# Stick-breaking attention: scores copied out of their bank by ScalarE, suffix sums added by VectorE, no second score matmul

## What is computed

```python
z = jnp.einsum('bqhd,bshd->bhqs', qb, k_b).astype(f32) * scale
strict = (key_pos[None, :] < t[:, None])[None, None]
log_1mb = jnp.where(strict, jax.nn.log_sigmoid(-z), 0.0)
after = lax.cumsum(log_1mb, axis=3, reverse=True) - log_1mb
att = jnp.where(strict, jnp.exp(jax.nn.log_sigmoid(z) + after), 0.0)
ob = jnp.einsum('bhqs,bshd->bqhd', att.astype(v_b.dtype), v_b)
```

## Time and profile before

| | us |
|---|---|
| median of 3 runs | 1699.08 |
| lowest, highest | 1697.08, 1699.22 |
| the profiled execution | 1696.48 |
| its span, first to last instruction | 1694.7 |
| TensorE busy | 1578.8 (93%) |
| VectorE busy | 840.5 (50%) |
| ScalarE busy | 624.2 (37%) |

### The profile page before, as it was taken

One profiled execution on the slowest core, in us unless ns is written; L12 is line 12 of the kernel. 1 busy time (PEld: TensorE's weight loads), 2 busy tenths in 40 slices (PEclk: granted clock), 3 DMA queues, 4 the chain that ended last, 5 costly groups with the idle time before them and its releaser, 6 DMA issues.

```text
span 1694.7 us, 22877 instructions
## 1 busy us (share of the span) xinstructions
PE 1578.8 (93%) x9177; PEld 1226.9 (72%) x9177; DVE 840.5 (50%) x1545; ACT 624.2 (37%) x1109; POOL 592.1 (35%) x452
## 2 busy tenths in 40 slices
PE   5899999999899988899899999998899899999997
PEld 4688766777788666677677776666677877877776
DVE  3779366333426356633518995455474533222224
ACT  4232365453322245443234324554353322221222
POOL 3445112234344321234233532211254354434441
PEclk9998999999999999999999999999999999999999
DMA  6867110122232210223132231100133232232221
GB/s 245 289 231 250 50 51 26 63 99 76 88 99 80 74 52 27 76 75 112 52 115 75 75 106 51 50 26 26 50 109 103 88 100 80 94 100 99 84 91 75
DMA packets 85290, 157.11 MB, mean 93 GB/s; under 512 B 2705, under 2 KB 20673, under 8 KB 85185
## 3 DMA queue, kind: packets, MB, share of 16 engines
q1 hardware_dynamic: 81184, 146.81, 26.0%
q10 hardware_dynamic: 4000, 8.84, 1.4%
HBM read 153.52 MB, written 2.12 MB: 92 GB/s over the span
## 4 chain that ended last, share of the span: by engine, by line
PE 76%; DVE 14%; ACT 4%; issue 3%; DMA 2%; POOL 2%; PEld 1%; SPq 0%; DVEq 0%; ACTq 0%; PEldq 0%
PE banks L371 10%; PE banks L373 9%; PE banks L372 9%; PE banks L367 8%; PE banks L369 8%; PE banks L368 8%; PE banks L467 4%; PE banks L469 3%; PE banks L468 3%; PE banks L492 2%; PE banks L507 2%; PE banks L517 2%; POOL w_lo L345 2%; ACT w_hi L863 1%; DMA w_raw<-att_w_in_dram 1%
## 5 line engine op out<-in xcount | busy, mean ns | idle before, releaser
L345 POOL TENSOR_TENSOR w_lo<-w_raw,w_hi 128x512 fp32r<-128x512 f32 x448 | 591.9, 1355 | 1071.9 <-ACT w_hi L863 1071.9
L863 ACT ACTIVATE w_hi<-w_raw 128x2048 fp32r<-128x2048 f32 (+1 forms) x114 | 214.6, 1882 | 221.0 <-DMA w_raw<-w_ff_dram 152.5
L367 PE MATMUL banks<-xh,w_hi 128*128 128x512 f32 x640 | 252.7, 395 | 5.1 <-issue 4.0
L369 PE MATMUL banks<-xh,w_lo 128*128 128x512 f32 x640 | 250.3, 391 | 0.0
L368 PE MATMUL banks<-xl,w_hi 128*128 128x512 f32 x640 | 250.3, 391 | 0.0
L371 PE MATMUL banks<-w_hi,xh 128*128 128x512 f32 x384 | 157.8, 411 | 25.3 <-POOL w_lo L345 12.9
L371 PE MATMUL banks<-w_hi,yh 128*128 128x512 f32 x384 | 151.7, 395 | 7.0 <-issue 4.2
L373 PE MATMUL banks<-w_hi,xl 128*128 128x512 f32 x384 | 153.4, 400 | 0.0
L372 PE MATMUL banks<-w_lo,xh 128*128 128x512 f32 x384 | 153.2, 399 | 0.0
L372 PE MATMUL banks<-w_lo,yh 128*128 128x512 f32 x384 | 149.8, 390 | 0.0
L373 PE MATMUL banks<-w_hi,yl 128*128 128x512 f32 x384 | 149.8, 390 | 0.0
(11 more groups left out here) (307 smaller groups left out, 2432.7 us busy)
## 6 DMA issues: line engine op xcount, KB each, us to landing
w_raw<-w_ff_dram SPq DMA_DIRECT2D x32, 1024.0 KB, 5.3
w_raw<-w_in_dram SPq DMA_DIRECT2D x22, 1024.0 KB, 5.1
w_raw<-att_w_in_dram SPq DMA_DIRECT2D x16, 1024.0 KB, 8.0
work_hi<-w_ada_dram SPq DMA_DIRECT2D x16, 1024.0 KB, 7.5
w_raw<-rec_w_in_dram SPq DMA_DIRECT2D x16, 1024.0 KB, 5.2
work_lo<-w_ada_dram SPq DMA_DIRECT2D x8, 1024.0 KB, 5.9
w_raw<-ple_w_gate_dram SPq DMA_DIRECT2D x8, 1024.0 KB, 5.1
w_raw<-att_w_out_dram SPq DMA_DIRECT2D x4, 1024.0 KB, 5.1
```

Of the source, the lines that this page charges most:

```text
L345: ins = pool.tensor_tensor(wlo[s][:, k, :], raw[s][:, k, :], wh[s][:, k, :].bitcast(F32), ALU.subtract)
L367: pe.matmul(out, w_h, x_h, start=start, stop=False)
L369: return pe.matmul(out, w_l, x_h, start=False, stop=stop)
L863: act.activation(wh[s][:, 0:kn, :], raw[s][:, 0:kn, :], ACT.Copy).then_inc(w_split, 1)
```

## The change

The second score pass is gone. `stick_scores` loses its argument; `stick_sums` starts the bank with the first suffix-sum matmul. ScalarE gets a new function `stick_keep`, which copies the scores from their bank to `stk_at` in SBUF, after both readers of the scores are through (`stk_sp`) and, from the second pass on, after the previous output matmuls have read the old weights out of `stk_at` (`stk_o`). TensorE waits for these copies (`stk_kept`) before it overwrites the bank. VectorE masks the diagonal tiles in `stk_at`, then adds the whole bank to `stk_at` (384, 384 and 512 columns for each head), and only that addition releases `stk_arg`. The weights' exp then reads `stk_at` and writes it in place. The next pass's first scores wait for `stk_arg` of the unit rather than for `stk_att`.

```diff
-            def stick_scores(i, j, stop):
+            def stick_scores(i, j):
...
-                    mm = pe.matmul(unit_bank(e, j, j), ks[hs, j * P:j * P + P], qs[hs, j * P:T], start=True, stop=stop)
-                    if stop and j < 3:
+                    mm = pe.matmul(unit_bank(e, j, j), ks[hs, j * P:j * P + P], qs[hs, j * P:T], start=True, stop=True)
+                    if j < 3:
...
             def stick_first(i, u):
                 if i > 0:
-                    pe.wait_ge(sg("stk_att"), stk(i - 1, 1, u))
+                    pe.wait_ge(sg("stk_arg"), stk(i - 1, 1, u))
...
             def stick_sums(i, j):
                 pe.wait_ge(sg("stk_sp"), stk(i, 1, STK_UNIT[j][0]))
-                stick_scores(i, j, False)
+                pe.wait_ge(sg("stk_kept"), stk(i, 1, STK_UNIT[j][0]))
...
-                        pe.matmul(unit_bank(e, j, j2), tri if j2 == j else ones, stk_hi[e][u][:, cut], start=False, stop=False)
+                        pe.matmul(unit_bank(e, j, j2), tri if j2 == j else ones, stk_hi[e][u][:, cut], start=j2 == j, stop=False)
...
-                    act.activation(stk_at[e][u][:, 0:w], ps[:, 3 * e + u, 0:w], ACT.Exp).then_inc(sg("stk_att"), 1)
+                    act.activation(stk_at[e][u][:, 0:w], stk_at[e][u][:, 0:w], ACT.Exp).then_inc(sg("stk_att"), 1)
+
+            def stick_keep(i, u):
+                w = STK_COLS[u]
+                if i > 0:
+                    act.wait_ge(sg("stk_o"), i)
+                for e in range(2):
+                    act.wait_ge(sg("stk_sp"), stk(i, e, u))
+                    act.activation(stk_at[e][u][:, 0:w], ps[:, 3 * e + u, 0:w], ACT.Copy).then_inc(sg("stk_kept"), 1)
...
             def stick_masks(i, u):
+                w = STK_COLS[u]
                 for e in range(2):
+                    x = diagonals(stk_at[e][u], u)
+                    dve.wait_ge(sg("stk_kept"), stk(i, e, u))
+                    V.mark(dve.tensor_tensor(x, x, each(strict_neg, u), ALU.add))
+                V.wait()
+                for e in range(2):
+                    x = stk_at[e][u][:, 0:w]
                     dve.wait_ge(sg("stk_r"), stk(i, e, u))
-                    x = diagonals(ps[:, 3 * e + u, :], u)
-                    dve.tensor_tensor(x, x, each(strict_neg, u), ALU.add).then_inc(sg("stk_arg"), 1)
+                    dve.tensor_tensor(x, x, ps[:, 3 * e + u, 0:w], ALU.add).then_inc(sg("stk_arg"), 1)
```

More of the change, by code:

```diff
@@ L750, in stick_first @@
                 if i > 0:
-                    pe.wait_ge(sg("stk_att"), stk(i - 1, 1, u))
+                    pe.wait_ge(sg("stk_arg"), stk(i - 1, 1, u))
                 for j in [j for j in reversed(range(TT)) if STK_UNIT[j][0] == u]:
-                    stick_scores(i, j, True)
+                    stick_scores(i, j)
             def stick_sums(i, j):
                 pe.wait_ge(sg("stk_sp"), stk(i, 1, STK_UNIT[j][0]))
-                stick_scores(i, j, False)
+                pe.wait_ge(sg("stk_kept"), stk(i, 1, STK_UNIT[j][0]))
                 for e in range(2):
@@ L1227, in _ @@
                 stick_logs(i, 1)
+                stick_keep(i, 2)
                 stick_logs(i, 0)
+                stick_keep(i, 1)
+                stick_keep(i, 0)
                 for u in (2, 1, 0):
```

## The result

| | before | changed |
|---|---|---|
| median, us | 1698.08 (4 runs) | 1709.01 (4 runs) |
| lowest, highest | 1696.39, 1699.22 | 1707.98, 1710.29 |
| profiled execution, its span | 1696.48, 1694.7 | 1708.56, 1706.4 |

The changed kernel is slower: ratio 1.0066, interval [1.0048, 1.0083], 10.9 us by the medians. In a second measurement against 17 runs of the kernel before it took 1709.86 us (6 runs, one of them at 1715.50), ratio 1.0071, [1.0059, 1.0083].

A forecast was written before the change was run, and what follows sets the result against it. The prediction took VectorE's half of the stage's loop, not TensorE, as the bound: +2.5 us chain and +4.4 us clock falls gave +6.9 us, 1706.0 us against the median of 1699.08, range 1699.0 to 1711.0.

The forecast's parts named there:

- VectorE's half of the loop: In each stage pass, from the gb2 copy to VectorE's last split; claimed to set the pace while TensorE has slack.
- the removed 11.8 us of TensorE work: The second score passes, 2.95 us a pass over four passes, claimed to lie mostly in TensorE's slack.
- TensorE was the bound after all: Rival: the removed TensorE work shows fully (1687 us) or half (1693); 1687 to 1696, chance 0.07.
- The chain, +0.63 us a pass: VectorE and ScalarE ahead of unit 0's sums: +1.05 additions, +0.69 copy and handovers, -1.11 removed; +2.5 us in four passes.
- The additions: VectorE's two additions of unit 2 and a wait, ahead of unit 0's splits: +1.05 us a pass.
- the handovers: VectorE to ScalarE's unit 0 copy and on to TensorE's sums: two handovers, some 0.09 us together.
- ScalarE becomes the last: Rival: unit 0's logarithms run late, VectorE waits, four clock falls; +13 us, 1712; chance 0.13 together with more falls.
- The gap, 3.1 to 3.2 us: TensorE's idle time ahead of unit 0's sums, claimed to grow to this from 1.46 us.
- three falls of 1.45 us: TensorE's clock halved behind the gap ahead of unit 0's sums in three of four passes: 4.4 us.
- The rule that I used: All five TensorE gaps of 2.9 us and more in the earlier trace were followed by half clock.
- ScalarE last or more falls: Outcome class: VectorE waits for ScalarE's logarithms, or the clock falls more often; 1709 to 1714 us, chance 0.13.
- chain without the clock: Rival: TensorE's clock stays full in all or all but one pass; +2.5 to +4, 1701.6 us, chance 0.22.

The follow-up runs named there:

- the two filler pairs: Changed kernel without and with 12 idle matmuls a pass (1709.01, 1702.28 us); changed kernel with ScalarE's copies ahead of VectorE's splits, without and with them (1706.85, 1699.26).
- the filler: 12 idle matmuls a pass added to the changed kernel ahead of unit 0's sums: 1702.28 us against 1698.83 for the kernel before, ratio 1.0020.
- the kernel with the additions: Kernel before, second score pass kept, plus unit 2's two 384-column VectorE additions and one wait ahead of its masks: 1707.26 us against 1698.83.
- the kernels with both repairs: Changed kernel, ScalarE's copies ahead of VectorE's splits, masks and additions behind them: 1694.30 us; head 1, unit 2 split also ahead of gb2 copy: 1689.53.
- the one with the altered first pass: Previous kernel at 1689.53 us, but first-pass copies ahead of each unit's logarithms and its gb2 copy between the splits: 1688.62 us against 1698.38.
- the one with late masks: Changed kernel with unit 2's masks and additions moved behind unit 0's splits on VectorE: 1695.91 us against 1698.83, ratio 0.9983.
- all three kernels with a filler: Idle matmuls ahead of unit 0's sums: 12 in the changed kernel (1702.28 us), 12 with early ScalarE copies (1699.26), 6 in the 1688.62 us kernel (1687.96).

## Why the prediction was right

**The bound.** That VectorE's half of the loop, not TensorE, sets the pace held: 1.25 us a pass taken off its distance in the kernel before gave 5.9 us, while the removed 11.8 us of TensorE work gave nothing in the one kernel in which that half had its old length and the clock was kept (12.17 us of distance, gaps filled: 1699.26 against 1698.38). The rival "TensorE was the bound after all" fell.

**The chain, +0.63 us a pass.** Measured +0.72. The additions were right to the hundredth: 1148.63 to 1150.36 is 1.73 us for what took 0.67, so +1.06 against 1.05 forecast. The copy took its 0.60 (597 ns). What I mis-sized was the handovers, 0.09 us for both. From VectorE to ScalarE it took 1154.70 - 1154.66 = 0.04, and from ScalarE to TensorE, where the copy ends at 1155.30 and the sums start at 1155.44, 0.14: together 0.18. In four passes 2.9 us in place of 2.5. The rival "ScalarE becomes the last" fell: the logarithms of unit 0 started at 1145.58 in the second pass, head 0's were done some 2 us ahead of 1150.36, where VectorE takes them up, and VectorE had no wait for them in any pass.

**The gap, 3.1 to 3.2 us.** Measured 3.25 to 3.27, eight times in two profiles. The other gap that was forecast, about 1.5 us ahead of unit 1's sums, measured 1.51.

**The clock, three falls of 1.45 us.** Right in kind and proven apart from the chain by the two filler pairs. In size it was the term that was furthest off: not 4.4 us but 127.0 - 118.4 - 2.9 = 5.8 in the first profile (three passes, one of them for twice as long) and 6.6 in the second (four passes). Four stretches of 3.4 us at 1.45 to 1.65 us each. I had counted one fall off for the uncertainty of the gap, and a stretch could be twice as long, which I hadn't considered. The rule that I used, five of five from 2.9 us on, is not quite true: the first pass of the first profile kept its clock behind 3.26 us. Its list also left out a gap of 5.51 us that ends at 23.05 us of the kernel before. There the clock's row says 1.00, but the first matmul behind it took 0.79 us, as those at half clock do.

**The sum.** +6.9 forecast, +10.9 and +11.5 measured: 0.4 to the handovers, 1.4 to 2.2 to the clock, and the rest, 2 us, is outside the stage, part luck of the profile and part open. The range, 1699 to 1711, held both medians, but they lie above the band of 1704.5 to 1707.4 to which I gave 0.58. They fell among "ScalarE last or more falls", 0.13, of which the second half came true. The absolute time came out closer (3.0 us off) than the difference (4.0 off) by luck: with its fourth run the median of the kernel before came down by 1 us. The rival "chain without the clock" is what the filler made of it, 1702.28. For that I had 1701.6 "at the middle", which is the lower end; the middle of +2.5 to +4 is 1702.3.

**PSUM.** The rule of the Trainium skill, "PSUM — Partial Sum Buffer", section "PSUM bank collisions raise a hardware error", was never broken in a run, so none shows it. But my reading that by it the 0.60 us can't be hidden was too narrow: the copy can't run beside VectorE's read, yet it can run ahead of it, and then it is off the path (12.16 us). On the clock, the Trainium skill, "TensorE: Matmul & The Clock Gate", section "HAM oscillation — how this bites in real kernels", describes a kernel that loses its clock again at every wait of its loop. The runs agree in kind: the clock was lost in three of four passes in the first profile of the changed kernel and in all four in the second. That filling the wait ends it is what the runs with the filler show, at 1.00 behind the stage's entry.

## What to carry to other kernels

Work taken off an engine that waits inside a loop lengthens its wait; find the last instruction whose end starts the other half of the loop, and price the change by what it does to that instruction's end. On TensorE the longer wait can itself cost time, by the clock: here 12 idle matmuls a pass in a gap of over 3 us gave back 5 to 8 us. And before giving a half-idle engine more work, look at what stands behind that work in its order: the same two additions cost 8 us ahead of unit 0's splits, and behind them they left a distance of 11.17 us, in which they have no part.

## What the runs showed of the hardware

- Granted clock behind gaps ahead of unit 0's sums: 2.50 us was enough to lose it in three of four passes of the kernel with the additions; 3.26 us once was not. Of ten gaps of 1.63 to 1.65 us in the kernels with both repairs two were, both in the one with the altered first pass; of the eight of 1.45 to 1.55 us in the kernel before and in the one with late masks none was. At the stage's entry a gap of 1.52 us was followed by a fall in ten of fourteen profiles. The gap's length alone doesn't decide. Nor does the idle time of a pass: with late masks its waits of 0.87, 1.50 and 1.52 us add up to 3.9 us, and the clock was kept. What else does I can't say from these runs. In all three kernels with a filler the clock was kept behind the entry.
- One stretch of 3.4 us at half clock cost 1.45 to 1.65 us in TensorE's half of the loop and nothing where TensorE waits anyway. Where the clock was lost in the gap the first 512-column matmul of the changed kernel took 0.77 us, and 0.47 where it was kept.
- VectorE adds a bank to SBUF, 128x384 float32, in 550 ns and 128x512 in 687, about the same as its difference of two SBUF tiles (558 and 692).
- From the end of a ScalarE copy to the start of the matmul that waits for it are 0.14 us (1155.30 to 1155.44); from VectorE's low part to the matmul 0.06 (1150.83 to 1150.89 in the kernel before).
